# Two samples per matmul in the state update of an mLSTM head

## The reference

```python
C_new = decay[..., None, None] * C + jnp.einsum('bhs,bhsv,bhsk->bhvk', w_s, vc, kc)
```

## Time and profile before

| | |
|---|---|
| median of 3 runs | 931.23 us (931.2 to 931.47) |
| the profiled execution | 931.93 us |
| its span, first to last instruction | 930.4 us |
| mean granted TensorE clock | 0.995 |
| PE busy, share of the span | 98% |
| DVE busy, share of the span | 81% |
| ACT busy, share of the span | 51% |
| the state updates' matmuls (line 1521) | 64, in four heads |

### The profile page before, as it was taken

How to read it: one execution, slowest core, us unless ns; L and a number is a source line. 1 busy time by engine, 2 the same in 40 slices (tenths; PEclk the granted TensorE clock), 3 DMA queues, 4 the chain that set the end, 5 groups by cost and what they waited for, 6 DMA issues and landing times. The chain is left out here.

```text
span 930.4 us, 18155 instructions
## 1 busy us (share of the span) xinstructions
PE 916.2 (98%) x6801; PEld 902.2 (97%) x6801; DVE 756.0 (81%) x1186; ACT 472.6 (51%) x713; POOL 43.5 (5%) x70
## 2 busy tenths in 40 slices
PE   8999999999999999999999999999999999999996
PEld 8999999999999999999999999999999999999995
DVE  6899868886887797686265579999888999899997
ACT  7654552355346335625633345466445554556564
POOL 3011000000000000000240000000000000000001
PEclk9999999999999999999999999999999999999998
DMA  6245217311721452142532222422222222332122
GB/s 221 69 150 188 89 42 250 95 62 56 257 82 41 163 185 70 39 169 68 166 117 68 90 69 68 136 92 91 92 91 92 91 92 91 101 126 92 49 89 102
DMA packets 24108, 100.02 MB, mean 107 GB/s; under 512 B 3312, under 2 KB 6529, under 8 KB 19572
## 3 DMA queue, kind: packets, MB, share of 16 engines
q1 hardware_dynamic: 21240, 78.70, 26.0%
q0 software_dynamic: 1984, 19.72, 5.8%
q10 hardware_dynamic: 832, 0.88, 0.3%
HBM read 85.28 MB, written 12.44 MB: 105 GB/s over the span
## 5 line engine op out<-in xcount | busy, mean ns | idle before, releaser
L1336 PE MATMUL ps<-h_hi,w_hi 128*128 128x288 f32 x896 | 194.2, 298 | 1.4 <-DVE w_lo L1735 1.4
L1336 PE MATMUL ps<-h_hi,w_lo 128*128 128x288 f32 x896 | 191.7, 296 | 0.0
L1336 PE MATMUL ps<-h_lo,w_hi 128*128 128x288 f32 x896 | 191.5, 295 | 0.0
L805 ACT ACTIVATE w_hi<-raw 128x1024 fp32r<-128x1024 f32 x76 | 80.2, 1056 | 138.3 <-PE ps L1336 135.1
L1336 PEld LDWEIGHTS ps<-h_hi,w_hi 128*128 128x128 f32 x896 | 143.5, 189 | 2.6 <-issue 1.7
L1336 PEld LDWEIGHTS ps<-h_lo,w_hi 128*128 128x128 f32 x896 | 144.3, 189 | 0.0
L1336 PEld LDWEIGHTS ps<-h_hi,w_lo 128*128 128x128 f32 x896 | 144.1, 189 | 0.0
L1735 DVE TENSOR_TENSOR w_lo<-raw,w_hi 128x1024 fp32r<-128x1024 f32 x76 | 94.2, 1240 | 46.6 <-ACT w_hi L805 46.6
L1612 PE MATMUL ps<-cols_a,main 128*128 128x288 f32 x432 | 62.9, 295 | 0.1
L1612 PE MATMUL ps<-cols_b,late 128*128 128x288 f32 x432 | 62.8, 295 | 0.0
L1612 PE MATMUL ps<-cols_b,main 128*128 128x288 f32 x432 | 60.2, 295 | 0.2 <-issue 0.2
(11 more groups left out here) (379 smaller groups left out, 1792.1 us busy)
## 6 DMA issues: line engine op xcount, KB each, us to landing
raw<-w_head_in SPq DMA_DIRECT2D x40, 512.0 KB, 3.5
raw<-w_fp_in SPq DMA_DIRECT2D x18, 1024.0 KB, 5.0
cs<-st_c_in POOLq DMA_DIRECT2D x4, 2048.0 KB, 9.6
c_s_out<-cs POOLq DMA_DIRECT2D x4, 2048.0 KB, 7.4
raw<-w_fo_in SPq DMA_DIRECT2D x8, 1024.0 KB, 5.0
x<-xT_in SPq DMA_DIRECT2D x16, 288.0 KB, 4.3
raw<-w_cgcv_in SPq DMA_DIRECT2D x8, 512.0 KB, 3.8
raw<-w_ga_in SPq DMA_DIRECT2D x8, 512.0 KB, 3.5
```

Source lines behind the costliest of these rows:

```text
L805: act.activation(w_hi[:, s, :], raw[:, s, :], ACT.Copy).then_inc(hi_ready, 1)
L1336: last = pe.matmul(ps[:, 2 * s + b, 0:HALF], wt[:, w, k * P:k * P + P], src[:, k, b * HALF:b * HALF + HALF], start=(k == 0 and wt is w_hi ...
```

## The change

`state_update(u)` makes matmul u of 8 per head: two neighbouring samples (512 columns, a whole bank) for one half of the keys. Matmuls 2i and 2i + 1 hold samples 2i and 2i + 1. VectorE's update of sample b waits for the second matmul of the pair and reads two runs of 256, one in each of the two banks. TensorE, ahead of uses 24, 26 and 28, waits for the second sample of the pair that lay in the bank and its neighbour; ahead of 25 and 27 it has no wait. The order of VectorE's work, and all else, is as it was.

```diff
                     if k == 0:
                         pe.wait_ge(act_read, h * ACT_USES + START)
                         pe.wait_ge(dve_read, h * DVE_USES + START)
+                    elif CS_USE + 4 <= k <= N_USE:
+
+                        if (k - CS_USE) % 2 == 0:
+                            read(k - 3)
                     elif k >= 4:
                         read(k - 4)
...
-                def state_update(b):
-                    use(CS_USE + b)
-                    for k in range(2):
-                        last = pe.matmul(bank(CS_USE + b)[:, k * HD:k * HD + HD],
-                                         stk[0:3 * GT, b // SG, k * P:k * P + P],
-                                         wvs[b // SG][0:3 * GT, b % SG, :], start=True, stop=True)
-                    last.then_inc(attn_ready, 1)
+                def state_update(u):
+
+                    use(CS_USE + u)
+                    g, b, k = u // SG, u % SG // 2 * 2, u % 2
+                    pe.matmul(bank(CS_USE + u), stk[0:3 * GT, g, k * P:k * P + P],
+                              wvs[g][0:3 * GT, b:b + 2, :].rearrange("p s v -> p (s v)"), start=True, stop=True)\
+                      .then_inc(attn_ready, 1)
...
                 for b in range(SB):
-                    use(CS_USE + b)
-                    c = cs[:, b, :, :].rearrange("p k v -> p (k v)")
-                    dve.scalar_tensor_tensor(c, c, dec[:, bass.ds(h, 1), b:b + 1].rearrange("p o b -> p (o b)"),
-                                             bank(CS_USE + b), ALU.mult, ALU.add).then_inc(dve_read, 1)
+                    use(CS_USE + b // 2 * 2 + 1)
+                    at = 4 + (CS_USE + b // 2 * 2) % 4
+                    dve.scalar_tensor_tensor(cs[:, b, :, :], cs[:, b, :, :],
+                                             dec[:, bass.ds(h, 1), b:b + 1].rearrange("p o b -> p (o b)"),
+                                             ps[:, at:at + 2, b % 2 * HD:b % 2 * HD + HD], ALU.mult, ALU.add)\
+                       .then_inc(dve_read, 1)
```

## The result

The changed kernel takes 933.42 us (median of 14 runs, 932.4 to 934.1) against 931.29 us (14 runs, 930.63 to 931.95) of the kernel before beside it: a ratio of 1.0022, 95% interval 1.0015 to 1.0029. Measured again, the same pair gave 933.12 against 931.42, a ratio of 1.0019 (1.0010 to 1.0028). Both intervals leave out no change, so the kernel became slower, by some 0.2% (+1.4 to +2.7 us in the first, +0.9 to +2.6 in the second).

What follows compares the result with a forecast made beforehand. TensorE's instruction stream, busy 98%, was taken as the kernel's length. A 0.50 us stall per head, less 0.012 each for u = 6 and 7, gives +0.41, +1.6 us in all: 932.8 (own range 932.4 to 933.3; whole range 931.2 to 933.6).

Steps and rivals of the forecast that it cites:

- rival C: Two-bank access slows each VectorE update; at the bound of 0.05 us, +2.2 us, 933.4; chance 0.12.
- The first step: TensorE's waits in the whole run: the longest are 2.2 and 2.0 us, both outside the heads.
- Who waits for whom: Unit 8: VectorE's sample 2i waits for matmul 2i+1; TensorE's u = 4, u = 6 and L1529 wait for samples 1, 3, 5.
- VectorE's start: Unit 8: sample 0 waits for u = 1 and starts at 137.71 instead of 137.37, 0.34 us late.
- The two hand-overs: Unit 8: 0.16 us from a matmul's end to VectorE's start, 0.05 us from VectorE's end to the waiting weight load.
- The two-bank read: VectorE's update reads 2 x 256 elements in two banks instead of 512 in one; taken as costing nothing, 750 beside 750 ns.
- The second stall: After unit 8, L1529 waits for sample 5, ready at 144.61; TensorE gets there at 144.88, so no stall.
- The cover of what was moved: VectorE's 0.39 us delay stays hidden: over 1 us before TensorE's transposes, over twenty for the reload.
- s: Saving per step of unit 8 from one 512-column matmul for two of 256: 0.012 us, bounds 0 to 0.024.
- B: The wait hardly binds, VectorE not delayed: +0.02 us per head, 931.3, or 930.8 if it bound nowhere; chance 0.10.
- D: Wide matmuls nearly free, 0.132 us for 512 columns: 931.1, or 927.8 without the stall; chance 0.04.
- E: The wide matmul costs two halves, no saving per step: 933.1; chance 0.08.

Runs made afterwards that it cites:

- The last two runs: Kernel before with each 256-column update pair made three times, and changed kernel with each 512-column update made three times: 0.118 us per 256, 0.233 per 512.
- the run with 256 columns: Kernel before with each pair of 256-column updates made three times in a row: six take 0.71 us, 0.118 each; the step is 1.49 us.

## Why the prediction was right, and which term was off

The forecast was +1.6 us by one stall ahead of update 6 in each head, with +1.3 to +1.9 by the bounds of the columns' cost. The trace has +1.9, the timing +1.4 to +2.7. The chain of waits came as forecast; where the number fell is in part luck. The first median, 933.42, lies above the forecast's own 932.4 to 933.3 and inside the whole range, up to 933.6, only by the room left for rival C, which did not happen; the second, 933.12, lies inside both. By the prediction's own count a loss over 1.86 us had a chance of 0.28; the first measurement has 2.1, the second 1.7.

- The first step misread a row, without harm: the 2.0 us of the earlier trace rows are two waits, the longest 1.4, and that one lies inside head 0, in its third unit, ahead of unit 8. It goes into no term. In the kernel before:

```profile
80.09 0.53 PE L1336 MATMUL ps<-h_hi,w_hi 128*128 128x288 f32 x2 [1.45 <-DVE w_lo L1735]
```

- Who waits for whom: right, and shown. Each wait alone costs next to nothing, both with the old width cost the whole loss, and with the waits, the width and the two-bank reads kept the loss goes when the pair is made together or VectorE's other work is moved.
- VectorE's start: forecast 0.34 us late; it is (137.54 - 135.77) against (137.37 - 135.94), 1.77 against 1.43: 0.34.
- Sample 2 waits once more, for update 3: forecast 0.39 late in all. It starts 3.85 after the unit instead of 3.40, 0.45 late, because the steps didn't become shorter.
- The two hand-overs: VectorE to the load 0.05 us, as forecast; TensorE to VectorE 0.14 (137.40 to 137.54) for 0.16. The first matmul behind the wait is 0.10 longer (0.50 for 0.40), for 0.11.
- The two-bank read: taken at nothing. The 32 folds last 736 ns in the mean, against 732 before. A group that the change leaves alone went from 503 ns to 508 between the same two executions, so the 4 ns can't be put down to the read. VectorE's groups by form, before (first line) and in the changed kernel:

```profile
L2113 DVE SCALAR_TENSOR_TENSOR cs<-cs,dec,ps 128x512 f32<-128x512 f32 x32 | 23.4, 732 | 0.1
...
L2117 DVE SCALAR_TENSOR_TENSOR cs<-cs,dec,ps 128x512 f32<-128x512 f32 x32 | 23.5, 736 | 1.1 <-PE ps L1526 1.0
...
L2676 DVE SCALAR_TENSOR_TENSOR x<-x,vec,ps 128x288 f32<-128x288 f32 x4 | 1.9, 508 | 0.0
```

- The second stall: none in the changed kernel, as forecast; it came where the first was taken away (the run with the weights' part after sample 3).
- The cover of what was moved: held. The transposes after unit 9 start at 151.84, 0.32 later than before on the clock of the span, and no wait shows there.
- The term that failed is s, the gain of a step. It rested on the choice that the 0.012 us beyond the columns belong to an instruction. The last two runs show that, between these widths, they grow with the columns: 0.118 for 256, 0.233 for 512. So s is 2 x 0.118 - 0.233 = 0.003 us, not 0.012; and in the changed kernel the first steps of a unit became 1.04 instead of 1.03, for the 288-column matmuls behind a wide one are a little further apart. The walk with s = 0, which the prediction gave as a bound, ends at +1.9, where the trace is. That term was mis-sized, and the sum with it came out 0.3 us short.
- The prediction also worked out s = 0.022 by the Trainium skill, "TensorE: Matmul & The Clock Gate", section "Back-to-back issue gap". It set that section's price for 512 columns against the rows' 0.237 for the pair. With columns over 2.4 GHz plus 2.5 ns on both sides, the pair is an estimated 0.218, the wide one 0.216, and s 0.0025. The 0.003 of the runs agrees with this small gain, though not with the two prices.
- Rival by rival: B is out, for the waits are in the list; C, for the folds last 736 ns and not 0.05 us more, though its 933.4 is the nearest to the first median; D, for a wide matmul takes 0.233 us and not 0.132. E, that the wide matmul saves nothing over two halves, is what the columns do, and it holds beside the forecast's stall, not in its place: its 933.1 is the second median.

What stays open: why 288-column matmuls behind a 512-column one are some thousandths of a microsecond further apart in the first steps of a unit. No run was aimed at it.

## What to carry to other kernels

When one engine hands buffers to another, widening the unit of hand-over takes slack on both sides: the reader starts one step later, and the writer asks for a free buffer one step earlier. Either may be free alone, and both together may not, so walk the chain with both in it, through the reader's other work, and look for the one wait that ends last. Where a pair must be handed over as a pair, make its two halves together: the changed kernel with that done lost nothing. There the last pair was also made one block later (ahead of block 7, not 6), which gave VectorE more time; without that it was not run. Moving the reader's other work behind the sample that is waited for did the same here.

## What the runs showed of the hardware

From 256 to 512 columns a matmul in a full stream, at a granted clock of 1.00, cost nearly the same per column: 0.118 us for 256, about 0.13 for 288 ((138.84 - 138.06) / 6 in the run with 256 columns), 0.233 for 512. That is 0.45 to 0.46 ns per column, where one column per cycle of 2.4 GHz would be 0.42. It doesn't go on so below: the matmuls of L1533 and L1529 (plain float32, the others rounded parts) move 8 columns each, and two, three and four of them last 0.39, 0.50 and 0.61 us, 0.11 apiece. I had expected a fixed part per instruction, and so a gain from fewer instructions; halving the state updates' matmuls and weight loads, from 64 to 32, saved at most 0.2 us in all. The Trainium skill, "TensorE: Matmul & The Clock Gate", section "Back-to-back issue gap", gives columns over 2.4 GHz plus 2.5 ns as the isolated gap of one matmul, 0.216 us for 512, and 0.131 us for 512 in a sustained stream of loads and matmuls. The 0.233 us of the runs here agrees with neither.
